# One front stage over 512-token chunks in place of three: bias tables, index projection and index scores of a decoder layer

## What is computed

```python
z  = x @ w_in                                   # only the columns of qi, ki, wi matter to the front
wi = wi * (IDX_HEADS ** -0.5 * IDX_DIM ** -0.5) # 4 index heads, width 64
dots  = einsum('bqhd,bkd->bqhk', qi, ki)
score = einsum('bqh,bqhk->bqk', wi, relu(dots)) # causal, then top_k
logits = q.k * scale + rel_bias[t5_bucket(distance)]   # attention, later
```

## Time and profile before

| what | value |
|---|---|
| median of 3 runs | 5037.99 us (5034.23 to 5044.51) |
| profiled execution, first to last instruction | 5034.6 us (no other time of that execution is given) |
| PE busy | 3830.0 us, 76% of the span |
| DVE busy | 2735.9 us, 54% |
| ACT busy | 1465.2 us, 29% |
| start of `stage_select` | 459.25 us into the span |

### The profile page before, as it was taken

One profiled execution on the slowest core, in us unless ns is written; L12 is line 12 of the kernel. 1 busy time (PEld: TensorE's weight loads), 2 busy tenths in 40 slices (PEclk: granted clock), 3 DMA queues, 4 the chain that ended last, 5 costly groups with the idle time before them and its releaser, 6 DMA issues. The chain is left out here.

```text
span 5034.6 us, 41358 instructions
## 1 busy us (share of the span) xinstructions
PE 3830.0 (76%) x14920; PEld 2867.8 (57%) x14920; DVE 2735.9 (54%) x4193; ACT 1465.2 (29%) x1843; POOL 163.3 (3%) x153
## 2 busy tenths in 40 slices
PE   2498999960278788836758886999999759999995
PEld 2344777750145455514436665777777647777774
DVE  1045788787466665536655553544444454544545
ACT  1144634455233344423332221211211111121120
POOL 0000100100000000000000000000000000000000
PEclk9756999985578899956669997999999879999997
DMA  6211222210210100021124443111111021111110
GB/s 129 63 42 62 69 82 90 87 54 20 60 36 21 28 21 7 5 65 36 34 81 142 135 137 89 51 38 49 39 47 42 30 98 41 38 51 38 38 51 38
DMA packets 292641, 287.24 MB, mean 57 GB/s; under 512 B 34917, under 2 KB 248549, under 8 KB 287270
## 3 DMA queue, kind: packets, MB, share of 16 engines
q1 hardware_dynamic: 257934, 233.93, 16.2%
q10 hardware_dynamic: 31968, 42.47, 2.5%
q0 software_dynamic: 2560, 8.39, 0.6%
HBM read 209.25 MB, written 75.50 MB: 57 GB/s over the span
## 5 line engine op out<-in xcount | busy, mean ns | idle before, releaser
L88 PE MATMUL ffn_up<-ffn_xh,ffn_uh 128*128 128x512 f32 x1536 | 597.7, 389 | 3.5 <-DVE ffn_xl L1316 3.5
L89 PE MATMUL ffn_up<-ffn_xl,ffn_uh 128*128 128x512 f32 x1536 | 597.5, 389 | 0.0
L90 PE MATMUL ffn_up<-ffn_xh,ffn_ul 128*128 128x512 f32 x1536 | 597.5, 389 | 0.0
L88 PE MATMUL ffn_dn<-ffn_dh,ffn_hh 128*128 128x512 f32 x768 | 325.4, 424 | 156.2 <-DVE ffn_acc L1301 135.0
L1305 DVE TENSOR_TENSOR ffn_ul<-ffn_ur,ffn_uh 128x1024 fp32r<-128x1024 f32 x96 | 117.6, 1225 | 584.2 <-ACT ffn_uh L1256 584.2
L1301 DVE TENSOR_TENSOR ffn_acc<-ffn_dn,ffn_acc 128x1024 f32<-128x1024 f32 x192 | 232.8, 1222 | 288.0 <-PE ffn_dn L90 288.0
L428 ACT ACTIVATE sel_junk<-sel_scs,sel_cand 128x768 bf16<-128x768 f32 (+5 forms) x186 | 270.0, 1452 | 349.2 <-DVE sel_cand L509 348.2
L88 PE MATMUL sel_acc<-xhi,sel_whi 128*128 128x512 f32 x864 | 341.1, 395 | 37.7 <-POOL sel_wlo L450 37.7
L89 PE MATMUL sel_acc<-xlo,sel_whi 128*128 128x512 f32 x864 | 340.1, 394 | 0.0
L90 PE MATMUL sel_acc<-xhi,sel_wlo 128*128 128x512 f32 x864 | 339.5, 393 | 0.0
L88 PEld LDWEIGHTS ffn_up<-ffn_xh,ffn_uh 128*128 128x128 f32 x1536 | 288.3, 188 | 63.5 <-DVE ffn_xl L1316 3.9
(11 more groups left out here) (207 smaller groups left out, 7071.2 us busy)
## 6 DMA issues: line engine op xcount, KB each, us to landing
ffn_ur<-in_w_up_dram SPq DMA_DIRECT2D x96, 512.0 KB, 6.1
zt<-sel_out ACTq DMA_DIRECT2D x27, 1024.0 KB, 3.9
ffn_dr<-in_w_down_dram SPq DMA_DIRECT2D x48, 512.0 KB, 3.6
att_raw<-zt SPq DMA_DIRECT2D x64, 256.0 KB, 4.1
mrg_gr<-zt SPq DMA_DIRECT2D x64, 256.0 KB, 4.3
sel_wraw<-in_w_in_dram ACTq DMA_DIRECT2D x27, 512.0 KB
prj_xin<-in_x_dram SPq DMA_DIRECT2D x16, 512.0 KB, 5.3
yt<-att_y POOLq DMA_DIRECT2D x32, 256.0 KB, 2.8
```

The lines of the kernel that those rows point to most:

```text
L88: pe.matmul(out, ahi, bhi, start=first, stop=False)
L89: pe.matmul(out, ahi, blo, start=False, stop=False)
L90: return pe.matmul(out, alo, bhi, start=False, stop=last)
```

## The change

One stage, `stage_front` (`frt_`), does all of it.

- The tokens are taken in four chunks of 512. For chunk q the order, the same on every engine, is `tokens(q)` (8 transposed groups), then the index items of chunk q-1 in four portions, each followed by one step of `project(q, t)`: t = 0 and 1 are two query heads each, t = 2 the key and the head weights, t = 3 the transposes of the head weights. The items of chunk 3 (16 of them) come last. The portions for q = 1, 2, 3 are 1, 2 and 3 items (2, 8 and 12 items in all).
- ACT and DVE split the projections straight from PSUM into the SBUF operands `qst`, `khh` and `kl0`; nothing of the projection goes through `zt`. `kl0` (the low part of the key) has 128 rows, the upper 64 set to zero by POOL, so the second matmul of a head has 128 rows too and the same weights as the first.
- PSUM: two banks for transposed tokens (`ta`), two for projections (`pj`), four for `dots` (one for each head). Before, each stage had eight.
- Input tokens are loaded by halves of a block, four in flight (`RX = 4`).
- The rows of the bias table go to a small HBM tensor `brow`. The two transfers that repeat them into `bands` now read `brow`, are issued by ACT behind its part of `tokens(3)`, and only the attention waits for them (semaphore `bandst`).

```diff
+        ta = s.ps("ta", [P, 2, CH])
+        pj = s.ps("pj", [P, 2, CH])
+        dots = s.ps("dots", [P, 4, CH])
...
+        plan = [("tokens", 0, 0)] + [("project", 0, t) for t in range(4)]
+        for q in range(1, NCH):
+            plan.append(("tokens", q, 0))
+            own, per = of_chunk[q - 1], -(-len(of_chunk[q - 1]) // 4)
+            for t in range(4):
+                plan += [("index", q - 1, i) for i in own[t * per:(t + 1) * per]]
+                plan.append(("project", q, t))
+        plan += [("index", NCH - 1, i) for i in of_chunk[NCH - 1]]
...
 sync (SP):
+            sp.dma_start(brow, row[:]).then_inc(rowst, 16)
+            for op, q, i in plan:
+                if op == "tokens":
+                    for g in range(8 * q + RX, min(8 * q + 8 + RX, 2 * NB)):
+                        tokens(g)
+                elif op == "index":
...
+                    sp.dma_start(score[n, :, c * CH:c * CH + w], sc[:, i % 2, 0:w]).then_inc(st[i % 2], 16)
...
 scalar (ACT):
+                    for e in range(2):
+                        act.activation(qst[0:DH, q % 2, 2 * t + e, :], pj[e * DH:(e + 1) * DH, t, :], ACT.Copy).then_inc(qh, 1)
...
+                    if i:
+                        act.wait_ge(cmb, IDX_HEADS * (i - 1) + h + 1)
+                    act.activation(rl[:, h, 0:w], dots[:, h, 0:w], ACT.Relu).then_inc(re, 1)
...
+                    if q == NCH - 1:
+                        act.wait_ge(rowst, 16)
+                        for m in range(2):
+                            act.dma_start(bands[m], brow[:, m, :].rearrange("h (o d) -> h o d", o=1)
+                                          .broadcast_to([16, P, BAND])).then_inc(bandst, 16)
...
 vector (DVE):
+                if i >= 2:
+                    dve.wait_ge(st[i % 2], 16 * (i // 2))
...
 tensor (PE):
+                    if g < 2:
+                        pe.wait_ge(tabe, 1)
+                    else:
+                        pe.wait_ge(lo, g - 1)
...
+                    if i:
+                        pe.wait_ge(re, IDX_HEADS * (i - 1) + h + 1)
+                    qs = qst[:, (n // 4) % 2, h, (n % 4) * P:(n % 4 + 1) * P]
+                    pe.matmul(dots[:, h, 0:w], qs, khh[:, c * CH:c * CH + w], start=True, stop=False)
+                    pe.matmul(dots[:, h, 0:w], qs, kl0[:, c * CH:c * CH + w], start=False, stop=True).then_inc(mm, 1)
...
 attention:
+            sp.wait_ge(bandst, 32)
```

More of the change, by code:

```diff
@@ L90, in split3 @@
     return pe.matmul(out, alo, bhi, start=False, stop=last)
[L93 to L97, removed]
-        row = s.sb("row", [16, 2, BAND], F32)
[L99 to L128, removed]
@@ L131, in stage_project @@
[L131 to L211, removed]
@@ L214, in stage_index, with stage_front @@
[L214 to L221, removed]
+def stage_front(nc, x, w_in, rel, onehot, bands, brow, bandst, score, xhi, xlo, ident):
+    with Stage(nc, "frt") as s:
+        RX = 4
+        W3 = 2 * P + DH + IDX_HEADS
+        xin = s.sb("xin", [P, RX, CH], F32)
+        cols = [(0, P), (P, P), (2 * P, DH + IDX_HEADS)]
+        scr = s.sb("scr", [P, KT * W3], F32)
+        whi = s.sb("whi", [P, KT, W3], F32R)
+        wlo = s.sb("wlo", [P, KT, W3], F32R)
+        qst = s.sb("qst", [P, 2, IDX_HEADS, CH], F32R)
+        khh = s.sb("khh", [P, SEQ], F32R)
+        kl0 = s.sb("kl0", [P, SEQ], F32R)
+        row = s.sb("row", [16, 2, BAND], F32)
@@ L278, in _, with tokens @@
-            dve.wait_ge(wiv, 1)
-            dve.wait_ge(trid, 1)
-            links = 0
-            link = s.sem("link")
-            for i, (n, c, w) in enumerate(work):
+            links = 0
+            def tokens(q):
+                for g in range(8 * q, 8 * q + 8):
+                    b, half = g // 2, g % 2
+                    dve.wait_ge(hi, g + 1)
+                    dve.tensor_tensor(xlo[:, 4 * half:4 * half + 4, b * P:(b + 1) * P],
+                                      ta[:, g % 2, :].rearrange("p (j f) -> p j f", j=4),
+                                      f32(xhi[:, 4 * half:4 * half + 4, b * P:(b + 1) * P]), ALU.subtract).then_inc(lo, 1)
@@ L293, in _ @@
                     else:
[L294 to L302 removed]
+                        dve.wait_ge(cmb, IDX_HEADS * i + h)
@@ new lines, in index @@
+                        dve.scalar_tensor_tensor(o, rl[:, h, 0:w], wi[:, n, h:h + 1], o, ALU.mult, ALU.add).then_inc(cmb, 1)
+                if ends_row[i]:
+                    dve.wait_ge(cmb, IDX_HEADS * (i + 1))
+                    dve.tensor_tensor(sc[:, i % 2, w - P:w], sc[:, i % 2, w - P:w], tri[:], ALU.add).then_inc(dg, 1)
+            dve.wait_ge(tabm, 1)
+            dve.tensor_copy(row[:], ta[0:16, :, 0:BAND]).then_inc(tabe, 1)
+            for op, q, j in plan:
+                if op == "tokens":
+                    tokens(q)
+                    if q == 0:
+                        dve.wait_ge(whid, 1)
+                        dve.tensor_tensor(wlo[:], wraw, f32(whi[:]), ALU.subtract).then_inc(wlod, 1)
+                        dve.wait_ge(trid, 1)
+                elif op == "project":
+                    project(q, j)
+                else:
+                    index(j)
@@ L322, in stage_select @@
+            pe.wait_ge(ldt, 48)
+            for m in range(2):
+                last = pe.matmul(ta[0:16, m, 0:BAND], val[0:65, :], oh[:, m, :], start=True, stop=True)
+            last.then_inc(tabm, 1)
+            pe.wait_ge(kz, 1)
+            for op, q, j in plan:
+                if op == "tokens":
+                    tokens(q)
+                elif op == "project":
+                    project(q, j)
+                else:
+                    index(j)
 def stage_select(nc, w_in, zt, score, mask, xhi, xlo):
@@ L557, in _, with stage_attend @@
                     n_st += 16
-def stage_attend(nc, kind, zt, mask, bands, sinks, yt, ident):
+def stage_attend(nc, kind, zt, mask, bands, bandst, sinks, yt, ident):
     with Stage(nc, f"att{kind}") as s:
```

198 lines of the change are left out of this document (137 added, 61 removed).

## The result

The changed kernel takes 4819.3 us (median of 4 runs, 4813.8 to 4823.1) against 5041.3 (4 runs, 5034.2 to 5047.0): ratio 0.956, 95% interval 0.955 to 0.957. The profiled execution spans 4821.3 us. The forecast was 4831, its range 4795 to 4880.

What follows compares the result with a forecast made beforehand. Barrier-separated front stages: idle waits, and items set by PE at 5.4 us each. New chain 220.6 + 8 + 2.5 + 9 + 12 = 252 against 459.25, 207 less: 5034.6 - 207 = 4827.6, plus 3.4, 4831; range 4795 to 4880.

Steps and rivals of the forecast that it cites:

- 131 us with certainty: Front: waits for `bands` (65.7) and for `zt` out and back (8.7 + 57.0) go, on no new path.
- lower clock throughout: Rival, chance 0.13: projections and items of the new stage run at the lower clock, giving 4895 us.
- The rival in which items keep 5.4 us: Index items on PE stay at 5.4 us each despite 128 rows, total 4960 us; chance 0.03 within "lower clock throughout".
- the clock's 2 us a chunk: Projections behind transposes: the clock sinks while PE only transposes, costing 2 us for each of four stretches, 8 in all.
- the last items' 2.5: Last 16 items: PE needs only 1.65 of 2.8 us, so the clock may fall; 2.5 us, between 0 and 5.
- ACT's 9: ACT's issue of the `bands` transfers holds ACT, with relus, DVE and PE waiting: 9 us, bounds 0 and 10.
- the stores' 12: Score stores slowed beside the copy into `bands`, some 17 items within 64 us: 12 us, bounds 0 and 22.
- The cycles of chunks 2 and 3: Item portion, projection step, copies and last subtraction: cycles of 10.0 and 11.8 us, three per chunk, 30.9 and 36.
- starved stores: Rival, chance 0.15: a whole batch of copy rows passes ahead of each score store, 27 to 61 us, total 4846 to 4880.
- Token groups: 1.06 us each forecast: Token stretches: with two PSUM banks PE, ACT and DVE follow each other, 2.12 us for two groups, 8.5 a chunk.
- signs of being wrong: PE's clock staying at 0.50 in projections, token groups well over 1.1 us each, or stages behind select's start moving.
- clean: Rival, chance 0.17: the issue doesn't block and the copy from HBM is light, giving 4805 us.

Runs made afterwards that it cites:

- run 4: Kernel before, table rows sent to `brow`, both transfers into `bands` issued by ACT behind the tokens and awaited only by the attention: 4978.5 us, ratio 0.988.
- run 3: Kernel before with 128 rows for the low part of the key and each head's relu buffer released head by head: 4943.7 us, ratio 0.981.
- run 1: Changed kernel with the second matmul of each head back on 64 rows: 4901.0 us, ratio 0.973.
- run 2: Kernel before with only the low part of the key filled with zeros to 128 rows: 4976.0 us, ratio 0.987.
- run 6: Changed kernel with ACT's two transfers into `bands` moved from behind tokens(3) to chunk 0: 4813.2 us, ratio 0.955.
- run 5: Kernel before with only the source of the copy into `bands` changed to `brow`, still waited for: 4998.0 us, ratio 0.993.
- run 8: Changed kernel with the transfers into `bands` in chunk 0 and four PSUM banks for transposed tokens: 4803.0 us, ratio 0.953.
- run 9: Changed kernel with the transfers into `bands` in chunk 0 and the next chunk's token groups set between projection matmuls: 4802.1 us, ratio 0.953.
- run 10: Kernel of run 9 with one transfer into `bands` behind token group 15 and one behind group 23: 4799.3 us, ratio 0.953.

## Why the prediction was right

**The border.** All 216.1 us lie ahead of select's first load, and the 4578 us behind it stayed within 3 us: as argued.

**What goes.** "131 us with certainty" counted the three waits, and that holds as a floor. The runs give the shares of the 216.1 us that parts bring alone: 63.8 for the bands' wait (run 4), 94.9 for the items (run 3). The remaining 57.4 are what is left to the single stage: `zt` out and back (65.7), and the overlap, less what the new order costs. This last number is a difference, not measured alone, and it takes for granted that the two parts add.

**The forms.** The prediction read 5.4 us an item as the alternation at the lower clock, 0.72 against 0.43 us a matmul, and runs 1 and 2 show it in both directions. Of the clock it said only, against its rival "lower clock throughout", that the items of 0.50 had alternated forms; the runs show the two tied together. At the upper level the alternation alone would leave some 3.2 us an item (206 x 0.43/0.72 / 38, an estimate), close to DVE's 2.9: most of the 5.4 came of the lower clock. The rival in which items keep 5.4 us is out.

**The chain, piece by piece**, forecast with the clock's 2 us a chunk and the last items' 2.5, without ACT's 9 and the stores' 12:

| piece | forecast | measured |
|---|---|---|
| tables to the copy's end | 8.8 | 10.5 |
| tokens(0), weights | 9.7 | 11.3 |
| chunk 0 with tokens(1) | 34 | 36.4 |
| chunk 1 with tokens(2) | 32.5 | 33.4 |
| chunk 2 with tokens(3) | 47 | 46.2 |
| chunk 3 | 47 | 55.6 |
| last 16 items | 49.5 | 46.5 |
| to select's load | 2.6 | 3.3 |
| ACT held, stores | 21 | in chunk 3 and the last items |
| sum | 252.1 | 243.2 |

The sum is 8.9 below the forecast's, and it is that close because errors cancel. With the 9.3 us of run 6 for the last line but one, that line was 11.7 too dear, the last items 3.0 and chunk 2 0.8; the other pieces were 6.6 too cheap together. (The cycles of chunks 2 and 3 also add up to 30.0 and 35.4, where the prediction has 30.9 and 36.) The first pieces are over: the tables' matmuls start at 6.77 us, where they started at 5.08, behind more loads (timeline of PE). Chunk 3 holds ACT's 3.6 us and 8.2 of waiting for stores, yet run 6 wins only 9.3 there, so some 2.5 of them lay in time in which DVE would have idled anyway. The two terms in the last line but one were both too dear.

**ACT held by the issue: 9 forecast, 3.6 measured.** The 9.17 us were SP's with a source of 16 SBUF rows. From `brow` the second issue takes 2.98 us on ACT and 2.72 on SP (run 5): the queue blocks, as assumed, but for less time. In runs 6, 8 and 9, where token loads are under way beside it, it takes 5.0 to 5.3 us, though the two transfers of run 6 land as fast on average as those of the changed kernel (20.6 and 20.4 us). What sets its length was not isolated.

**Stores beside the copy: 12 forecast, 8.5 measured**, and both factors were wrong. I had 17 stores in 64 us, each landing in 4.1 us. The copy lasted 26 us, four stores fell into it, and three of them took 6.0 to 10.1 us. A store beside the copy was starved far more than forecast, for a shorter time than forecast. By the Trainium skill's rule (DMA: Bandwidth & Descriptors, Queues, rings and completion order), engines change queues by whole packets of rows; as the rival "starved stores" it gave 2.3 to 4.3 us a store on top. The three landings do not bear the amount out. At the rate measured, 25.9 us for 256 rows an engine, 0.10 us a row, 9 to 17 rows would be 0.9 to 1.7 us, and the two slow stores of 256 KB took 7.4 and 8.0 more than alone, while a fourth landed in 3.4. What held them is open. The rival's sum of 27 to 61 us did not come, because only four stores met the copy: its rate from HBM was in no row before, and the prediction had only "may be quicker".

**Token groups: 1.06 us each forecast, 1.30 measured** at the lower clock. DVE's timeline:

```profile
48.91 0.69 DVE L234 TENSOR_TENSOR xlo<-frt_ta,xhi 128x512 fp32r<-128x512 f32 x1 [1.49 <-ACT xhi L179]
49.76 0.69 DVE L234 TENSOR_TENSOR xlo<-frt_ta,xhi 128x512 fp32r<-128x512 f32 x1 [0.16 <-ACT xhi L179]
51.51 0.69 DVE L234 TENSOR_TENSOR xlo<-frt_ta,xhi 128x512 fp32r<-128x512 f32 x1 [1.05 <-ACT xhi L179]
```

Two groups every 2.60 us: PE's 0.54 and its restart stand on the chain, and were priced from rows at the upper clock. The term for the clock, 2 us a chunk, had thought of the projection's start alone. That costs about 1.4 us (seven matmuls 0.20 us dearer, last section), the tokens 4 x 0.48 = 1.9: 3.3 in place of 2. It is this step that failed, by little; chunks 0 and 1 are 2.4 and 0.9 over. Of the signs of being wrong that the prediction names (groups of well over 1.1 us), this one came.

**The clock.** 24 projection matmuls of 5.6 us at the upper level came; in chunk 0 the first 3.1 us of the projection ran at the lower. "Lower clock throughout" did not come: 0.90 to 0.96 in the mixed stretches.

**The last items: 45 + 2 + 2.5 forecast, 46.5 measured.** They are DVE's, 2.9 us each. The clock term was not needed there.

**How the total came out 12 below.** The front gave 8.9 more than forecast, the part behind took 2.8 more, and the median lies 2.0 below the profiled span where 3.4 above was assumed: 8.9 - 2.8 + 5.4 = 11.5. The last of these is scatter. The rival "clean", 4805, took issue and stores for nothing; run 6, which nearly makes them so, came to 4813. The measured 4819 lies about half-way between that rival and the forecast, and the total does not tell them apart; the 3.6 us of issue and the slow stores do.

## What to carry to other kernels

When a bound is removed, list what it was hiding before you price the next one: here the matmuls' forms hid a buffer given back too late, worth 30 us, and only the two edits together made the items DVE's. Don't alternate matmuls of 128 and 64 rows: filling the 64 up with zeros cost nothing on PE here and won 64 us in the kernel before. A small block that a broadcast repeats is better read from HBM than from a few SBUF rows, 24 against 64 us here; moving the wait off the path and speeding the copy are separate gains, and the second takes only a small transfer ahead of the copy. And place a large transfer where nothing small is awaited beside it: behind the tokens of chunk 0 it cost next to nothing, beside the score stores some 9 us.

## What the runs showed of the hardware that was not expected

- A broadcast copy of 6.29 MB in rows of 1536 bytes went at 243 GB/s over its whole length from HBM (25.9 us, beside other work; 293 GB/s in mid-copy with nothing beside it), and at 96 GB/s from 16 SBUF partitions. The issue of its second half held the issuing engine 2.7 to 3.1 us, against 9.2, on SP and on ACT alike, and 5.0 to 5.3 beside token loads (runs 6, 8 and 9); with 28 us between the halves the issues took 0.5 and 0.6 (run 10).
- Three of the four stores issued beside that copy, 256 KB and less, took 6.0 to 10.1 us to land, where 2.1 is usual for 256 KB.
- Alternating 128-row and 64-row matmuls of 512 columns start 0.43 us apart at the upper level and 0.72 at the lower, where one form alone starts 0.23 and 0.43 apart. And long rows of alternating matmuls ran at 0.50 with PE busy nearly all the time (203.7 of 206 us before, 62.5 of 64 in run 1), where the same items in one form ran at 0.84 to 0.94.
- The granted clock reads 1.00 from the start of the record, while the first matmuls of the projection start 0.43 us apart, as at the lower level. PE's timeline of the changed kernel:

```profile
28.65 0.63 PE L75 MATMUL frt_pj<-xhi,frt_wlo 128*128 128x512 f32 x1
29.07 0.62 PE L73 MATMUL frt_pj<-xhi,frt_whi 128*128 128x512 f32 x1
29.50 0.42 PE L74 MATMUL frt_pj<-xlo,frt_whi 128*128 128x512 f32 x1
29.76 0.39 PE L75 MATMUL frt_pj<-xhi,frt_wlo 128*128 128x512 f32 x1
30.00 0.39 PE L73 MATMUL frt_pj<-xhi,frt_whi 128*128 128x512 f32 x1
```

Before the first change of level that the record holds, the spacing of matmuls tells the level better than the clock's column.
- The same eight token groups behind the same neighbours ran at 0.50 in one kernel (2.60 us a pair) and at the upper level in another whose only difference is the copy's place (2.13 us). What decides between them stayed open.
